# A new order of the stages of the RWKV-7 chunk scan: both Gram products first, and the chain's solving, output and state stages between crossing and growing

## The reference

```python
def rwkv7_scan(r, w, k, v, kk, a, s0):
    def step(s, inp):
        rt, wt, kt, vt, kkt, at = inp
        sa = jnp.einsum('nbhij,nbhj->nbhi', s, kkt)
        s = (s * wt[..., None, :] - sa[..., :, None] * (kkt * at)[..., None, :]
             + vt[..., :, None] * kt[..., None, :])
        return s, jnp.einsum('nbhij,nbhj->nbhi', s, rt)
```

## Time and profile before

| | |
|---|---|
| median of 3 runs | 5158.94 us (5129.7 to 5165.66) |
| the profiled execution | 5144.95 us, span 5143.4 us |
| PE busy (matmul) | 4324.6 us, 84% |
| PE busy (weight load) | 2941.5 us, 57% |
| DVE, ACT, POOL busy | 43%, 24%, 30% |
| the scans | about 1470 to 3130 us after the start |
| PE busy in 250 us slices of the scans | 219 to 226 us |

### The profile page before, as it was taken

The page is one execution under the profiler, slowest core; times in us unless marked ns, Lnnn a source line. Parts: engine busy times, 40 slices in busy tenths (PEclk is TensorE's granted clock), DMA queues, the critical chain, the costliest instruction groups (busy, mean ns, idle before and its releaser), DMA issues. The chain is left out here.

```text
span 5143.4 us, 122709 instructions
## 1 busy us (share of the span) xinstructions
PE 4324.6 (84%) x47298; PEld 2941.5 (57%) x47298; DVE 2215.9 (43%) x4008; ACT 1248.8 (24%) x3133; POOL 1565.5 (30%) x1949
## 2 busy tenths in 40 slices
PE   3999889999968888888888895875699999988990
PEld 1877766666657777777787783443233333333330
DVE  1111167676744555555454454887111111111118
ACT  0000044444423333333233332221000000000002
POOL 0000001111134645555455563442222222212224
PEclk7999999999989999999899997887799999999995
DMA  9311256566533232222322225342766888889766
GB/s 296 148 61 52 67 174 205 189 203 199 173 92 92 73 93 73 89 68 66 92 72 89 61 72 168 136 133 77 282 266 274 333 347 344 362 365 403 316 259 269
DMA packets 303064, 916.96 MB, mean 178 GB/s; under 512 B 70544, under 2 KB 169232, under 8 KB 269616
## 3 DMA queue, kind: packets, MB, share of 16 engines
q1 hardware_dynamic: 247760, 759.97, 41.3%
q0 software_dynamic: 47392, 133.02, 7.2%
q10 hardware_dynamic: 7488, 17.83, 0.9%
HBM read 951.09 MB, written 211.26 MB: 226 GB/s over the span
## 5 line engine op out<-in xcount | busy, mean ns | idle before, releaser
L2423 PE MATMUL exp_gate_up<-exp_w_gate,exp_rows_and_rowsT 128*64 128x512 f32 x1664 | 766.7, 619 | 90.9 <-DMA exp_w_up<-in_moe_w_up_dram 90.0
L2423 PE MATMUL exp_gate_up<-exp_w_up,exp_rows_and_rowsT 128*64 128x512 f32 x1664 | 767.5, 620 | 0.0
L2423 PEld LDWEIGHTS exp_gate_up<-exp_w_gate,exp_rows_and_rowsT 128*64 128x64 f32 x1664 | 234.6, 143 | 588.3 <-issue 588.3
L1554 POOL TENSOR_TENSOR rw_A_level<-rw_A_rho_beta,const_level_masks 128x256 f32<-128x256 f32 x432 | 340.4, 804 | 644.8 <-DVE rw_A_rho_beta L1570 386.9
L721 PE MATMUL rwp_product<-rwp_hT,rwp_w_rw 128*128 128x256 f32 (+1 forms) x2016 | 442.2, 382 | 0.0
L2375 DVE TENSOR_TENSOR exp_hidden<-exp_hidden,exp_gate_up 64x512 f32<-64x512 f32 x104 | 71.9, 692 | 816.4 <-ACT exp_hidden L2356 816.4
L721 PEld LDWEIGHTS rwp_product<-rwp_hT,rwp_w_rw 128*128 128x128 f32 (+1 forms) x2016 | 379.5, 189 | 60.8
L874 PE MATMUL hgp_product<-hgp_hT,const_w_hg 128*128 128x256 f32 x1728 | 393.4, 383 | 15.8 <-DMA hgp_hT<-s_hT 15.8
L2447 PE MATMUL exp_down<-exp_w_down,exp_hiddenT 128*64 128x512 f32 x1664 | 380.0, 598 | 1.1
L874 PEld LDWEIGHTS hgp_product<-hgp_hT,const_w_hg 128*128 128x128 f32 x1728 | 326.3, 192 | 70.4 <-DMA hgp_hT<-s_hT 16.3
L1585 DVE TENSOR_TENSOR rw_inverse<-rw_inverse,rw_inverse_bank 128x512 f32<-128x512 f32 x288 | 196.6, 684 | 344.3 <-PE rw_inverse_bank L1464 343.2
(11 more groups left out here) (384 smaller groups left out, 7925.4 us busy)
## 6 DMA issues: line engine op xcount, KB each, us to landing
exp_w_gate<-in_moe_w_gate_dram SPq DMA_DIRECT2D x104, 2048.0 KB
exp_w_up<-in_moe_w_up_dram SPq DMA_DIRECT2D x104, 2048.0 KB
exp_w_down<-in_moe_w_down_dram SPq DMA_DIRECT2D x104, 2048.0 KB
s_rw_in<-prep_operands SPq DMA_DIRECT2D x72, 514.0 KB, 4.1
rw_operands<-s_rw_in SPq DMA_DIRECT2D x72, 514.0 KB, 4.7
rw_tokens<-s_rw_tm SPq DMA_DIRECT2D x144, 192.0 KB, 5.8
hg_qkf<-s_hg_in SPq DMA_DIRECT2D x36, 768.0 KB, 7.5
mod_w<-in_w_mod_dram SPq DMA_DIRECT2D x24, 1024.0 KB, 26.1
```

What stands on the lines that cost most here:

```text
L1554: nc.gpsimd.tensor_tensor(self.al[d][l % 2][:], self.ar[u][d][:, :, 0, :], self.K["lvc"][:, d, l, :].unsqueeze(1).broadcast_to([P, NPAIR, ...
L2423: i = nc.tensor.matmul(pgu[u][q:q + BLK], xT[:, k, r * BLK:(r + 1) * BLK], w[r][:, k, :], start=(k == 0), stop=(k == KD - 1))
```

## The change

Only the table is edited.

```diff
-RW_ORDER = ("gram0 rhs gram1 turn cross1 solve grow1 cross2 out grow2 cross3 grow3 state cross4 grow4 cross5 grow5").split()
+RW_ORDER = ("gram0 gram1 rhs turn cross1 grow1 cross2 solve grow2 cross3 out grow3 cross4 state grow4 cross5 grow5").split()
```

## The result

The changed kernel takes 5221.69 us (median of 4 runs, 5209.33 to 5234.72), the kernel before 5158.46 beside it. The ratio is 1.013, with a 95% interval of 1.0104 to 1.0156. It is slower by more than the 1% that the prediction called within reach of a measurement, and above the range. The profiled execution is one of 5230.83 us, 86 above the one profiled before, though the medians are 63 apart. Both single executions lie on the outer side of their medians, so differences of the two traces are somewhat too large for the median.

The account below looks back on a forecast made before the run. PE's queue was taken to bound the kernel, through its waits and clock. Per round +0.4 in step A and -0.37 in step B, over 18 rounds about +1 us: 5146 profiled, 5160 by median, named 5152, range 5112 to 5190.

Parts of the forecast that it names:

- a step B 0.37 us shorter: Step B: crosses -0.68, `cross4` without cover +0.61, `grow4` -0.3; sum -0.37 us a round, ends -0.7 and +0.1.
- The prediction's own sign of being wrong: Scans: rounds over 2 us longer or shorter; also no wait above 1 us from `grow2` to `grow3`, or clock below 0.94.
- The wait moves one stage forward: Step A: PE's wait at `grow3` moves to `cross3` of direction 1, behind DVE's scans: 2.92 us, about 0.5 longer.
- `out` at 21.90: Step A: `cross3` ends at 19.10, `out` takes 2.80 and ends at 21.90; `grow3` then starts, net +0.56 us.
- a rival of +15 us: Scans: a clock fall in every round where about half have one now, 9 x 1.7 = +15 us, 5161; chance 0.09.
- So `s_ready` comes 0.4 later: End of step A: `state` 1.50 us later, DVE's update and step B's loads only 0.4 later; ends 0 and 1.5.
- the claim that DVE takes up 1.1 us of the move: End of step A: DVE has done other work earlier, so `state` +1.50 us makes `s_ready` only 0.4 later.
- load of step B decides: Rival: DVE absorbs nothing of `state`'s delay, loads +1.5 us a round, +20 us in all, 5165; chance 0.13.
- Its gram 1 and rhs swap places with nothing gained: Step B's start: an HGRN2 score and turn stage cover the mask, so the swap changes nothing.
- The +0.33 counted in step A: Step A's start: gram 1 waits for its mask until 2.54, so `turn` starts at 6.20 instead of 5.87, +0.33 us.
- Time for fetching them is kept at nothing: Whole kernel: the number of instructions is the same, so fetching them adds no time.
- The "covered" rival: Step A: scans do not hold up `cross3`'s second direction; -26 us, up to 12 more, 5107 to 5119; chance 0.10.

Follow-up runs that it names:

- the experiment with `state` alone: The kernel before with `state` moved behind the fourth crossing and nothing else; ratio 1.0030 to the kernel before.
- Holding the loads: Changed kernel with the RWKV loads of each round's first step held until PE's last crossing of the step before; ratio 1.0033 to the kernel before.
- early loads: RWKV loads wait for PE's state product instead of DVE's update; on the changed kernel 1.0021, on the kernel before 0.9922, both to the kernel before.

## Why the prediction was wrong

The forecast was a sum of +1 us, made of a state that is ready 0.4 us later in step A and a step B 0.37 us shorter. The step that failed first is the one from `cross3` to the loads, and after it three terms that were put at nothing or nearly so. The prediction's own sign of being wrong, rounds over 2 us longer, is what came: in the traces a round is 4.7 us longer.

- **The wait moves one stage forward: right.** It said 2.92 us at the second direction of `cross3`, starting at 18.63; it was 3.07 at 19.05. The walk to that point holds: gram 1 at 2.54, `turn` 6.17 (6.20), `cross1` 7.49 (7.54), `solve` 12.18 (12.20), `cross3` of direction 0 at 15.30 (15.24). The 0.4 at the end are the scans: from their start to the addition behind them it was 2.74, not 2.26.
- **"`out` at 21.90", and with it all that follows: wrong by the clock.** The prediction took 2.80 for `out` at full clock and forecast `state` at 25.46. It was 27.47: 0.4 by the scans and 1.5 by `out` at the lower clock. The row that decided was in hand, the window of 0.62 in the earlier trace rows, and the text itself took "half" of the rounds, as a rival of +15 us and not as a term of the sum. The longer wait, with full work after it, brought a fall in every round. The page "TensorE: Matmul & The Clock Gate" of the Trainium skill, section "HAM oscillation — how this bites in real kernels", tells of a kernel in which a recurring wait of PE brings the clock down each time. The traces agree: falls in 17 of 17 rounds behind 3.07 us, in 10 of 17 behind 2.41.
- **"So `s_ready` comes 0.4 later": wrong, it was 2.7.** Of the 2.3 between, 2.0 is `state` later than forecast, and 0.3 the claim that DVE takes up 1.1 us of the move: in the changed kernel it took up 0.8 of 3.5, and in the experiment with `state` alone about a quarter where the prediction had nearly three quarters. So the 1.08 us of its operation was no sign of a queue that a later `state` would find empty. The rival "load of step B decides" had this term right (+1.5, 20 us; measured 15 for `state` alone) and got a chance of 0.13.
- **"Its gram 1 and rhs swap places with nothing gained": wrong for step B.** The +0.33 counted in step A was right (0.25 and 0.31). In one of the two steps B the swap cost 0.73 us. The part alone costs 0.44%, 23 us, over half of it in half-clock time of step B that no step of the sum covers.
- **"Time for fetching them is kept at nothing": wrong.** The number of instructions is the same, but PE's place at the moment of the loads is not. "Issue" at `grow` went from 5.1 to 19.8 us in 1000. In the first step B of the loop body half-clock time is 58 us; before it was 24, all in one fall at one stall of 2.0 us. Holding the loads gave back 1.0 points. That it is fetching rests on the argument above.
- **The "covered" rival, 5107 to 5119.** The order on DVE did exclude it, as the prediction says, and with the scans put behind the addition the stage is covered. But its own gain, 26 to 38 us under the kernel before, did not come: that kernel is 1.5 points faster than the changed one and only 6 us faster than the one before (0.9982, the interval takes in 1). Step A gained, and step B took it back. The whole of it came with the exponentials moved as well (0.9939, 29 us). A due time 0.001 of a round ahead in another table decided whether the stage was covered.
- **The sum** had terms of both signs that cancelled to +1 us. What it lacked was that each error adds: a later `state`, a later load, a stall at the wrong moment, most of them with a fall of the clock behind. In the traces a step A is 2.9 us longer, where the forecast had 0.4, and a step B 1.8 us longer, where it had 0.37 less. The chance of 0.82 for a change within 1% rested on the clock and the load as rivals of 15 and 20 us, either the one or the other. The clock came to about 24 of the 63 us, and the three parts cost 23, 15 and 26 us by themselves; all came together.

## What to carry to other kernels

When stages are moved to cover a wait, walk the queue of the engine that is waited for as well, and look for an operation that stands ahead of the needed one by a hair: here moving DVE's scans behind one addition was worth more (1.5 points) than the whole reordering of PE lost (1.3). Where a trace already shows the clock falling behind a wait of 2 to 3 us, price every such wait in every round with a fall, and add what the fall delays. Loads that wait for the last reader of a buffer should wait for that reader alone: 16 bytes a row had held back 2 KB pieces by a DVE update, for 0.8% of the kernel.

## What the runs showed of the hardware

- PE can stall with nothing to wait for when data loads go out at the wrong moment. With the RWKV loads (1.8 MB by the page's DMA issues) going out 4 to 6 us ahead of an instruction packet, PE stalled 2.0 to 2.55 us in seven of eight rounds and 1.2 in the eighth. With the loads held 4.6 us longer it did not stall there, though the DMA engines were then 84% busy.
- Behind those seven stalls the clock fell, for 3 to 14 us (up to 24 in other kernels), although PE was busy nearly all of that time (14.68 of 15.00 us in the window above). Behind the one of 1.2 us it did not. With early loads the stalls were 0.9 to 2.0 us, and one fall followed in eight rounds. Why some falls last much longer than others stays open; the stage in which they last is HGRN2's output.
- 48 matmuls of no use in a wait of 3 us (x96 in the trace) made the kernel 0.9 points faster.
- One kernel's runs differ by their clock: the 31 runs of the kernel before lie between 5136.81 us at 0.928 and 5190.56 us at 0.920. So two single executions can lie 50 us apart with nothing changed.
